# An expert stage of 32 passes: where VectorE copies a pass's tokens, and when the sum banks are cleared

## The reference

```python
# every token has 2 of 32 experts; xb: the tokens of one expert, w_buf: their weights
def expert_block(args):
    xbk, e = args
    return (jax.nn.silu(xbk @ w_gate[e]) * (xbk @ w_up[e])) @ w_down[e]

yb = lax.map(expert_block, (xb, block_e)).reshape(P, D)
y = jnp.zeros((N + 1, D), yb.dtype).at[tok_buf].add(yb * w_buf[:, None].astype(yb.dtype))
```

## Time and profile before

| | us |
|---|---|
| three runs | 1620.1, 1614.2, 1610.67 |
| median | 1614.2 |
| the profiled execution, its own time | 1613.56 |
| its span, first to last instruction | 1611.8 |
| TensorE matmul busy in the span | 1522.3 (94%) |
| VectorE busy | 416.2 (26%) |
| ScalarE busy | 230.3 (14%) |
| mean granted clock of TensorE | 0.989 of 2.4 GHz |
| HBM read | 398.66 MB, 248 GB/s over the span |

### The profile page before, as it was taken

How to read it: one execution, slowest core, us unless ns; L and a number is a source line. 1 busy time by engine, 2 the same in 40 slices (tenths; PEclk the granted TensorE clock), 3 DMA queues, 4 the chain that set the end, 5 groups by cost and what they waited for, 6 DMA issues and landing times.

```text
span 1611.8 us, 20683 instructions
## 1 busy us (share of the span) xinstructions
PE 1522.3 (94%) x8032; PEld 968.8 (60%) x8033; DVE 416.2 (26%) x809; ACT 230.3 (14%) x463; POOL 21.5 (1%) x68
## 2 busy tenths in 40 slices
PE   4999999999999999999799999999989999999998
PEld 2766795544444444444484547777768644777775
DVE  1355564511111111111300422111130062211112
ACT  1230000410000000000301621000030042200001
POOL 2000000000000000000000000000000000000000
PEclk9999999999999999999899999999999999999999
DMA  9565503699999999999963853444264485144420
GB/s 368 206 249 209 210 1 154 251 369 424 422 414 425 426 426 428 427 424 427 399 228 122 341 194 131 157 157 156 78 249 169 157 323 190 61 157 157 156 78 26
DMA packets 89091, 400.72 MB, mean 249 GB/s; under 512 B 6688, under 2 KB 11936, under 8 KB 62912
## 3 DMA queue, kind: packets, MB, share of 16 engines
q1 hardware_dynamic: 89024, 399.73, 62.8%
HBM read 398.66 MB, written 1.05 MB: 248 GB/s over the span
## 4 chain that ended last, share of the span: by engine, by line
PE 77%; DMA 11%; DVE 5%; issue 2%; DVEq 2%; ACT 2%; SPq 0%; ACTq 0%
PE psum L1261 19%; PE psum L972 10%; DMA ring<-in_moe_up 10%; PE psum L1274 9%; PE psum L1091 7%; PE psum L584 4%; PE psum L1224 3%; PE psum L1112 3%; PE psum L521 3%; PE psum L960 2%; DMA ring<-in_ada_w 1%; PE psum L716 1%; PE psum L734 1%; PE psum L728 1%; PE psum L920 1%
## 5 line engine op out<-in xcount | busy, mean ns | idle before, releaser
L972 PE MATMUL psum<-ring,arena 128*64 128x256 f32 (+1 forms) x2400 | 326.9, 425 | 23.5 <-DMA ring<-in_moe_up 14.3
L1261 PE MATMUL psum<-arena,ring 128*128 128x256 f32 x1408 | 312.1, 380 | 0.1
L1261 PEld LDWEIGHTS psum<-arena,ring 128*128 128x128 f32 x1408 | 268.0, 191 | 54.1 <-issue 19.5
L972 PEld LDWEIGHTS psum<-ring,arena 128*64 128x64 f32 x2400 | 173.0, 137 | 186.3 <-issue 78.5
L1274 PE MATMUL psum<-ring,arena 128*128 128x512 f32 x352 | 157.9, 592 | 0.0
L1091 PE MATMUL psum<-arena,ring 128*128 128x256 f32 x512 | 112.0, 381 | 0.5 <-DVE arena L1364 0.4
L1926 DVE TENSOR_SCALAR arena<-psum,cols 128x256 f32<-128x256 f32 x44 | 23.9, 544 | 324.4 <-PE psum L1261 324.4
L1274 PEld LDWEIGHTS psum<-ring,arena 128*128 128x128 f32 x352 | 66.9, 190 | 66.3 <-issue 63.6
L1091 PEld LDWEIGHTS psum<-arena,ring 128*128 128x128 f32 x512 | 97.7, 191 | 14.4 <-issue 1.1
L1721 DVE TENSOR_TENSOR arena<-psum,arena 128x256 f32<-128x256 f32 x32 | 13.6, 424 | 255.5 <-PE psum L972 255.5
L960 PE MATMUL psum<-arena 64*128 64x512 f32 x272 | 76.2, 639 | 2.1 <-ACTq L2120 1.4
(11 more groups left out here) (379 smaller groups left out, 1218.2 us busy)
## 6 DMA issues: line engine op xcount, KB each, us to landing
ring<-in_moe_gate SPq DMA_DIRECT2D x30, 2048.0 KB, 20.7
ring<-in_moe_up SPq DMA_DIRECT2D x30, 2048.0 KB, 19.2
ring<-in_moe_down SPq DMA_DIRECT2D x30, 2048.0 KB, 20.8
ring<-in_w_mod SPq DMA_DIRECT2D x24, 2048.0 KB, 7.6
ring<-in_ada_w SPq DMA_DIRECT2D x12, 2048.0 KB, 10.7
ring<-in_w_qkv SPq DMA_DIRECT2D x12, 2048.0 KB, 18.4
ring<-in_w_ffn_gate SPq DMA_DIRECT2D x10, 2048.0 KB, 7.8
ring<-in_w_ffn_up SPq DMA_DIRECT2D x10, 2048.0 KB, 12.5
```

Of the source, the lines that this page charges most:

```text
L972: ins = mm(bank[b][o, 0:n], lhsT, w[:, half * n:(half + 1) * n], start=first, stop=last, tile_position=(0, 64 * half))
L1261: last = mm(b[:, k * TOK:(k + 1) * TOK], sl[k][2][:, c, j * P:(j + 1) * P], hTd[:, c, :], start=(c == 0), stop=(c == DC - 1))
```

## The change

VectorE's copy of tokens moves from the head of its turn to a place behind the activation product, and copies the tokens of the pass that follows (`following` is the next expert's first slot, a fourth register; for the last expert it reads the entry behind the first slots, and nobody reads what is copied). The first pass's tokens are copied once ahead of the loop, with an own wait for the gather copies. The wait for `up_done` at the head goes; the product's wait for `up_done` of its own pass covers it. On TensorE three of the four clearing products move ahead of the wait for the last gather copy, in the order of banks 5, 6, 7, 4; the waits for ScalarE's `ym_ready` and VectorE's `pwin_made` at that place are replaced by one for GpSimd's zeros.

```diff
             def gathered():
 
-                pe.wait_ge(S("xs_copied"), 8)
+                pe.wait_ge(S("iota_made"), 3)
                 pe.wait_ge(S("routes_copied"), 2)
+                for k in (1, 2, 3, 0):
+                    if k == 0:
+                        pe.wait_ge(S("xs_copied"), 8)
+                    hs = slice(64 * (k % 2), 64 * (k % 2) + 64)
+                    mm(bank[4 + k][:, :], pwin[hs, 0:P], ym[hs, :], start=True, stop=False, skip_group_check=True)
                 for name in ("up_done", "down_done", "act_turned"):
                     pe.nop().then_inc(S(name), 1)
-                pe.wait_ge(S("ym_ready"), 1)
-                pe.wait_ge(S("pwin_made"), 1)
-                for t in range(NT):
-                    add_y(t, first=True)
...
+            dve.wait_ge(S("xs_copied"), 8)
+            V.tensor_copy(xw, xsT[:, :, 0:WIN]).then_inc(S("xw_ready"), 1)
+
+            def act_pass(following, row, done):
 
-                dve.wait_ge(S("up_done"), done)
-                V.tensor_copy(xw, xsT[:, :, bass.ds(start, WIN)]).then_inc(S("xw_ready"), 1)
                 dve.wait_ge(S("silu_done"), done + 1)
                 dve.wait_ge(S("up_done"), done + 1)
                 dve.wait_ge(S("act_turned"), done)
                 V.tensor_tensor(actm, bank[2][:, 0:4 * WIN], sg, ALU.mult).then_inc(S("act_done"), 1)
+                V.tensor_copy(xw, xsT[:, :, bass.ds(following, WIN)]).then_inc(S("xw_ready"), 1)
                 dve.wait_ge(S("act_turned"), done + 1)
                 dve.wait_ge(S("down_done"), done)
...
                 start = dve.value_load(mtab[0:1, bass.ds(i, 1)], min_val=0, max_val=SLOTS)
+                following = dve.value_load(mtab[0:1, bass.ds(i + 1, 1)], min_val=0, max_val=SLOTS)
```

More of the change, by code:

```diff
@@ L945, in gathered, with add_y @@
             def gathered():
-                pe.wait_ge(S("xs_copied"), 8)
+                pe.wait_ge(S("iota_made"), 3)
                 pe.wait_ge(S("routes_copied"), 2)
+                for k in (1, 2, 3, 0):
[3 more added lines that the diff above has]
+                    mm(bank[4 + k][:, :], pwin[hs, 0:P], ym[hs, :], start=True, stop=False, skip_group_check=True)
                 for name in ("up_done", "down_done", "act_turned"):
                     pe.nop().then_inc(S(name), 1)
-                pe.wait_ge(S("ym_ready"), 1)
-                pe.wait_ge(S("pwin_made"), 1)
-                for t in range(NT):
-                    add_y(t, first=True)
-            def add_y(t, first=False, name=None):
+            def add_y(t, name=None):
                 for n in range(2):
                     hs = slice(64 * n, 64 * n + 64)
-                    last = mm(bank[4 + 2 * t + n][:, :], pwin[hs, t * P:(t + 1) * P], ym[hs, :], start=first,
+                    last = mm(bank[4 + 2 * t + n][:, :], pwin[hs, t * P:(t + 1) * P], ym[hs, :], start=False,
                               stop=(name is not None), skip_group_check=True)
@@ L1712, in _ @@
             dve.wait_ge(S("routes_copied"), 2)
-            def act_pass(start, row, done):
-                dve.wait_ge(S("up_done"), done)
-                V.tensor_copy(xw, xsT[:, :, bass.ds(start, WIN)]).then_inc(S("xw_ready"), 1)
+            dve.wait_ge(S("xs_copied"), 8)
+            V.tensor_copy(xw, xsT[:, :, 0:WIN]).then_inc(S("xw_ready"), 1)
+            def act_pass(following, row, done):
                 dve.wait_ge(S("silu_done"), done + 1)
@@ L1737, in _ @@
                     with dve.Fori(0, extra, 1) as w:
-                        act_pass(nc.s_assert_within(start + w * WIN, 0, SLOTS, skip_runtime_bounds_check_because=within),
+                        act_pass(nc.s_assert_within(start + w * WIN + WIN, 0, SLOTS, skip_runtime_bounds_check_because=within),
                                  nc.s_assert_within(i * 4 + w, 0, 4 * NE - 1, skip_runtime_bounds_check_because=within),
                                  before + w)
-                act_pass(nc.s_assert_within(start + extra * WIN, 0, SLOTS, skip_runtime_bounds_check_because=within),
+                act_pass(nc.s_assert_within(following, 0, SLOTS, skip_runtime_bounds_check_because=within),
                          nc.s_assert_within(i * 4 + extra, 0, 4 * NE - 1, skip_runtime_bounds_check_because=within),
```

## The result

Over 20 runs of each, the kernel after takes 1623.07 us in the median (1617.95 to 1630.5) and the kernel before 1616.75 us (1610.67 to 1627.78): a ratio of 1.0041, 95% interval 1.0027 to 1.0055. The change costs 6.3 us, where 1.6 were to be won. The kernel before's median over 20 runs is also 2.6 us above the one of three runs that the prediction started from.

A forecast was written before the change was run, and what follows sets the result against it. The stage was taken as bound by DMA at 426 GB/s plus two holes. TensorE gains 0.15 + 1.5 = 1.65 us at the second, 1.6 reach the end: 1612.6 us from 1614.2, range 1609.0 to 1617.5 (0.92).

The forecast's parts named there:

- part 1's price for the wait on the token copy: At pass boundaries: TensorE idles 0.20 us for VectorE's token copy; moving the copy closes that gap, 1.5 us by 442.23.
- The slower rival: A second long branch in one of the first eight passes: 2.3 us of TensorE idle, 1614.9 us; chance 0.07.
- The gain of a pass: At each pass boundary: next products start when the down product ends, winning 0.2 us a pass.
- the second hole: DMA shortfall in 442 to 460 us, 394 GB/s, 1.35 us, from late issue; TensorE would be 1.65 us early there.
- The head: At the stage's start: TensorE's first register load and first product come 0.15 us earlier, as two waits go.
- the rival of the drained nops: At the head: nops wait for the queued clears, first product 0.8 us late; 1613.5 us; chance 0.05.
- the full head: At the head: the clears were the bound, so 1.9 us are won there; 1611.0 us; chance 0.07.
- The cover of the copy: In VectorE's turn behind the activation product: 0.3 us of cover, then 0.5 more, hide the moved token copy.

The follow-up runs named there:

- copy_only: Only the token copy's part of the change, against the kernel before, TensorE's code untouched; 1622.33 us, ratio 1.0035.
- held_by_ym: Kernel after, plus a TensorE wait at each pass's head for ScalarE's copy of the last down product; 1614.96 us, ratio 0.9997 against before.
- held_odd: Kernel after, plus a wait for ScalarE's copy of the last down product in passes of experts 1, 3, 5, 7, 9; 1613.76 us, 0.9976 against before.
- held_even: Kernel after, plus a wait for ScalarE's copy of the last down product in passes of experts 0, 2, 4, 6, 8; 1624.08 us, 1.0043 against before.
- slow_down: Kernel after, with token copy and a mask product put ahead of the copy the down product needs; 1629.43 us, ratio 1.0087 against before.
- before_front63: Kernel before, plus 63 nops at the very start of TensorE's program; 1614.61 us, ratio 0.9991 against before.

## Why the prediction was wrong

**The step that failed is part 1's price for the wait on the token copy.** The prediction read that wait as 0.20 us of TensorE's idle time and as nothing else. The wait stands at the head of TensorE's pass, and it also kept TensorE's sequencer from going on until the tokens were there. Let go early, the sequencer meets the branches of experts 2, 6, 8 and 10 without their code, four times in both profiles after against once and twice before, and TensorE idles 2.15 to 3.73 us at each. The step said "TensorE's own register loads don't stop that", and asked only whether the sequencer is ready in time; what else it does when it is let go early was not asked. The runs put the loss on that: copy_only has it with TensorE's program untouched, held_by_ym takes it away with the change kept, and held_odd against held_even shows in which passes.

**The slower rival had the right place and the wrong mechanism.** It named the branch of an early pass and 2.3 us of idle time. But it made added and moved instructions the cause, and one instruction either way did nothing to the time. It allowed for one long branch more, where the profile has three more, and it had no price for the clock, 1.7 us behind each of three.

**The Trainium skill's rule** ("Runtime: NRT & Kernel Launch", "Instruction fetch mechanics") fits what was seen. The DMA view of a pass ahead of a short branch, before from 341.1 to 354.5, and of the same pass after, ahead of the long one:

```profile
q8 instruction: 2, 0.03, 0.9%
```

```profile
q8 instruction: 1, 0.02, 0.4%
```

A packet of code of 16 KB that came inside the pass before is missing after, and comes only at 356.8, 3.1 us after the branch began (353.66), while data hold the DMA engines at over 400 GB/s. By the rule the branch must fetch its target, and the records agree. The rows give its price: the branch took 4.4 us before and up to 5.5 us after.

**The gain of a pass was mis-sized, the right way.** Forecast were 0.2 us; it was 0.43. The idle time of 0.20 is about half of it; the rest is taken to be products that now overlap across the seam, which no run separates. The 1.65 us at the second hole never arrived. What the change is worth with no stall at all isn't known: in the one pair without long branches the stage gained 0.3 us, with short gaps in their place.

**The head was right.** The first product comes 2.71 us behind the last gather copy, 2.90 before: 0.19 us won, forecast 0.15. The three nops ran from 326.9 to 327.2 while the clears were under way until 327.99, so a nop doesn't wait for the matmuls queued ahead of it: the rival of the drained nops falls, and so does that of the full head. **The cover of the copy was right** too: the down product still begins 9.6 us behind its pass's start. **The second hole** was TensorE's doing, as forecast, but it grew from 1.35 to 5.7 us: idle gaps of 3.62, 2.15 and 2.39 us, all ahead of it or in it, made the loads late. The gate matrix issued at 442.23 before was issued at 450.80 after.

**The base was a low draw.** Three runs with a median of 1614.2 stood for a kernel at 1616.75, and the profiled execution, 3.2 us below that, had one long branch where a second profile had two. The range was set around it, and its upper end at 1617.5 left no case that moves several branches.

**What stays open.** Why the second packet of code fails to come when the first is late in the pass wasn't settled, nor what makes the first late in expert 1's pass even behind a hold, nor why 32 instructions more make the stalls more and shorter, at no cost in time. Code without the branch over the extra passes was not tried.

## What to carry to other kernels

A wait that costs 0.2 us of idle time may hold a sequencer back, and that may be worth more than the wait costs: before removing it, look at which branches the engine will reach earlier, and whether any of them has ever been long. A branch that took 20 times its median once is a stall that a harmless edit can multiply, so take several profiles and count such rows in each. Where passes are paced by loads, TensorE time won or lost in every pass is worth little (held_by_ym, below), while a few stalls ahead of that stretch delay the loads themselves.

## What the runs showed of the hardware

A nop on TensorE's sequencer takes 0.154 us from one to the next, three times its recorded 51 ns. The clock doesn't fall in every gap: after 3.62 and 2.39 us of idle time the next products took 8.81 us, after 2.15 us they took 7.13, and so they did after 3.21 us in slow_down:

```profile
453.24 7.13 PE L973 MATMUL psum<-ring,arena 128*64 128x256 f32 x64 [3.21 <-issue]
```

And a stage whose passes take 14.0 us instead of 13.48 (held_by_ym against before_front63) is only 1.4 us longer, 455.5 against 454.1 us, since loads set its pace: both move 426 GB/s from 460 to 769 us.
